# The low half of each weight gets a place of its own in the written order

## The reference, cut to what matters

```python
def reference(x, ...):
    x = first_block(x, ...)     # per layer: rms_norm, h @ w_in, two kinds of attention with
                                # relative bias, @ w_out, then conv_ffn (h @ w_up, causal
                                # conv of width 3, silu(g) * up, @ w_down)
    return second_block(x, ...) # per layer: adaptive rms_norm, h @ w_in of 15 sections (conv
                                # branch, attention with rope, gated linear attention with a
                                # chunked scan), three gated branches, @ w_out, rms_norm
```

## Time and profile before

| what | value |
|---|---|
| median of 3 executions | 2046.79 us (2045.48 to 2047.96) |
| the profiled execution | 2051.6 us |
| its span, first to last instruction | 2049.8 us |
| mean granted TensorE clock | 0.996 |
| TensorE busy | 2009.4 us (98%) |
| VectorE busy | 1330.0 us (65%) |
| ScalarE busy | 955.7 us (47%) |
| GpSimd busy | 159.3 us (8%) |

### The profile page before, as it was taken

One profiled execution on the slowest core, in us unless ns is written; L12 is line 12 of the kernel. 1 busy time (PEld: TensorE's weight loads), 2 busy tenths in 40 slices (PEclk: granted clock), 3 DMA queues, 4 the chain that ended last, 5 costly groups with the idle time before them and its releaser, 6 DMA issues.

```text
span 2049.8 us, 33452 instructions
## 1 busy us (share of the span) xinstructions
PE 2009.4 (98%) x13114; PEld 1738.3 (85%) x13114; DVE 1330.0 (65%) x2339; ACT 955.7 (47%) x1574; POOL 159.3 (8%) x169
## 2 busy tenths in 40 slices
PE   9999999999999999999999999999999999999998
PEld 7779998878999888888888788888878899888997
DVE  6767667767877337476445555868566686575665
ACT  4655555565555434353432453233246454445444
POOL 2001000000110100000200001111110000100100
PEclk9999999999999999999999999999999999999999
DMA  8446665535555322222222104534234244441554
GB/s 248 148 142 245 228 225 196 181 108 175 186 176 191 137 93 81 75 83 83 72 93 93 52 31 157 193 116 161 92 129 154 93 135 155 134 154 57 193 172 134
DMA packets 79706, 285.54 MB, mean 139 GB/s; under 512 B 8976, under 2 KB 9644, under 8 KB 79552
## 3 DMA queue, kind: packets, MB, share of 16 engines
q1 hardware_dynamic: 71136, 256.93, 37.7%
q10 hardware_dynamic: 6416, 19.51, 2.7%
q0 software_dynamic: 2000, 6.97, 1.3%
HBM read 277.55 MB, written 5.83 MB: 138 GB/s over the span
## 4 chain that ended last, share of the span: by engine, by line
PE 81%; DVE 10%; ACT 6%; issue 2%; DMA 1%; POOL 0%; ACTq 0%; DVEq 0%; SPq 0%
PE pb L1124 16%; PE pb L1126 15%; PE pb L1125 15%; PE pb L1137 6%; PE pb L1139 6%; PE pb L1138 6%; DVE SPL L2222 3%; ACT SPH L1637 3%; PE pb L1143 3%; PE pb L1302 2%; PE pb L1496 2%; PE pb L1303 2%; PE pb L1304 2%; PE pb L1477 2%; PE pb L1391 1%
## 5 line engine op out<-in xcount | busy, mean ns | idle before, releaser
L2222 DVE TENSOR_TENSOR SPL<-RAW,SPH 128x1024 fp32r<-128x1024 f32 x460 | 558.9, 1232 | 367.2 <-ACT SPH L1637 343.4
L1637 ACT ACTIVATE SPH<-RAW 128x1024 fp32r<-128x1024 f32 x462 | 477.4, 1052 | 208.4 <-PE pb L1126 111.3
L1124 PE MATMUL pb<-HTH,SPH 128*128 128x256 f32 (+1 forms) x1304 | 447.0, 343 | 8.4 <-POOL HTL L2881 3.1
L1126 PE MATMUL pb<-HTH,SPL 128*128 128x256 f32 (+1 forms) x1304 | 437.9, 336 | 0.0
L1125 PE MATMUL pb<-HTL,SPH 128*128 128x256 f32 (+1 forms) x1304 | 437.5, 335 | 0.0
L1124 PEld LDWEIGHTS pb<-HTH,SPH 128*128 128x128 f32 x1304 | 247.8, 190 | 36.8 <-ACT HTH L1686 3.2
L1126 PEld LDWEIGHTS pb<-HTH,SPL 128*128 128x128 f32 x1304 | 247.8, 190 | 26.1
L1125 PEld LDWEIGHTS pb<-HTL,SPH 128*128 128x128 f32 x1304 | 248.0, 190 | 24.8
L1137 PE MATMUL pb<-SPH,HTH 128*128 128x512 f32 x640 | 254.6, 398 | 2.1 <-DVE SPL L2222 1.4
L1139 PE MATMUL pb<-SPL,HTH 128*128 128x512 f32 x640 | 249.9, 390 | 0.0
L1138 PE MATMUL pb<-SPH,HTL 128*128 128x512 f32 x640 | 249.8, 390 | 0.0
(11 more groups left out here) (297 smaller groups left out, 2853.2 us busy)
## 6 DMA issues: line engine op xcount, KB each, us to landing
RAW<-in_w_up SPq DMA_DIRECT2D x88, 512.0 KB, 4.5
RAW<-in_wa SPq DMA_DIRECT2D x64, 512.0 KB, 3.5
RAW<-in_w_in SPq DMA_DIRECT2D x48, 512.0 KB, 4.7
RAW<-in_wmg SPq DMA_DIRECT2D x48, 512.0 KB, 3.5
RAW<-in_wbr SPq DMA_DIRECT2D x48, 512.0 KB, 3.5
RAW<-in_w_down SPq DMA_DIRECT2D x44, 512.0 KB, 4.9
RAW<-in_w_ada SPq DMA_DIRECT2D x24, 512.0 KB, 4.7
ARAW<-in_w_ada ACTq DMA_DIRECT2D x24, 512.0 KB, 4.2
```

The source lines that it names most:

```text
L1124: T.matmul(o, wh[:, kt, :], xh[:, kt, n0:n1], start=kt == 0, stop=False)
L1126: m = T.matmul(o, wl[:, kt, :], xh[:, kt, n0:n1], start=False, stop=kt == 7)
L1637: A.activation(hi, raw, ACT.Copy, scale=1.0).then_inc(*act.tick(s["hi"], ("u", u)))
L2222: W.tensor_tensor(lo, raw, hi.bitcast(F32), SUB).then_inc(*dve.tick(s["lo_dve"], ("u", u)))
```

## The change

The step `split` is now ScalarE's alone. VectorE (and POOL, where a fetch is its) has a step `split_low`. `split_upto` still adds `split` where it did, and notes the fetch as pending. `get_w(u)` first adds the low halves that are pending from the fetch before (`lows()`), then calls `split_upto` in its later form, which leaves the new ones pending; if u itself is among them, they are added at once. Every other call of `split_upto` adds its low halves at its end, as before.

So the low half of a fetch that `get_w(u)` starts is written one fetch later: behind the products of fetch u and behind all steps up to the next `get_w`. The high halves, the loads and TensorE's steps keep their order. No instruction is added or taken away.

```diff
+        self.later, self.pending = True, []
...
+    def lows(self):
+        for u in self.pending:
+            self.add("split_low", u)
+        self.pending = []
+
+    def split_upto(self, n, later=False):
         while self.order is not None and self.splits <= n and self.splits < len(self.order):
             u = self.splits
             self.load_upto(u + NR - 1)
             if u not in self.loaded:
-                return
+                break
             if self.order[u][3] == "split":
                 q = self.nsplit % NS
                 if q in self.held:
-                    return
+                    break
                 self.held.add(q)
...
                 self.add("split", u)
+                self.pending.append(u)
             self.splits += 1
+        if not later:
+            self.lows()
...
         if self.order is not None:
             assert self.order[u] == (name, idx, cols, kind)
-            self.split_upto(min(u + NS + 1, self.limit))
+            self.lows()
+            self.split_upto(min(u + NS + 1, self.limit), self.later)
+            if u in self.pending:
+                self.lows()
         return u
...
-    does = {"start": start, "cs": cs, "lam": lam, "split": split, "ada_turn": ada_turn, ...
+    does = {"start": start, "cs": cs, "lam": lam, "split_low": split, "ada_turn": ada_turn, ...
...
-    does = {"start": start, "qk_turn": qk_turn, "split": split, "bias_rows": bias_rows, ...
+    does = {"start": start, "qk_turn": qk_turn, "split_low": split, "bias_rows": bias_rows, ...
```

More of the change, by code:

```diff
@@ L183, in load_upto @@
             self.loads += 1
-    def split_upto(self, n):
+    def lows(self):
[3 more added lines that the diff above has]
+    def split_upto(self, n, later=False):
         while self.order is not None and self.splits <= n and self.splits < len(self.order):
@@ L2797, in x_out @@
             *dve.tick(o, ("x", l, t)))
-    does = {"start": start, "cs": cs, "lam": lam, "split": split, "ada_turn": ada_turn, "adv": adv, "adv_end": adv_end,
+    does = {"start": start, "cs": cs, "lam": lam, "split_low": split, "ada_turn": ada_turn, "adv": adv, "adv_end": adv_end,
             "adv_fin": adv_fin, "stats": stats, "scale": scale, "prod": prod, "bias_rows": bias_rows, "mask": mask, "picks": picks,
@@ L2944, in x_back @@
                     ).then_inc(*pool.tick(s["x_back"]))
-    does = {"start": start, "qk_turn": qk_turn, "split": split, "bias_rows": bias_rows, "consts": consts, "ctx_in": ctx_in,
+    does = {"start": start, "qk_turn": qk_turn, "split_low": split, "bias_rows": bias_rows, "consts": consts, "ctx_in": ctx_in,
             "bias_back": bias_back, "prod": prod, "up": up, "keep": keep, "gnorm": gnorm,
```

## The result

The change makes the kernel slower. Measured: 2059.15 us (median of 4 executions, 2058.14 to 2064.08) against 2046.13 (median of 4, 2044.27 to 2047.96); the ratio is 1.007, with an interval of 1.0058 to 1.0082. I had forecast slower, but 2052 with a range up to 2059: 5.2 us of +13.0. The profiled execution of after took 2058.1 us, 6.5 more than that of before (2051.6), and that distance is only half of what the medians give; the experiments come back to it.

A forecast was written before the change was run, and what follows sets the result against it. TensorE, busy 98% of the span, was taken as the bound almost everywhere. Gains of -14.5 and losses of +19.8 gave +5.3 us, 2056.9 against the profiled execution or 2052 against the median, range 2044 to 2059.

The forecast's parts named there:

- Item (6): First section of layer 0: fetch 4's low half, behind `qk_sums` and `qk_scale`, stalls TensorE from 25.73 to 31.75, +6.0 us.
- Item (7): Low granted clock after the stall at layer 0's first section: +2.4 us, with ends 0 and 3.4.
- The sum: Whole kernel: gains -14.5 plus losses +19.8 make +5.3 us, so 2052 against the median; chance 0.55.
- Item (10): Feed-forward of layer 1: late low halves of fetches 165 (+1.7) and 168 (+2.7), four fetches behind `prod c0` +1.6 us.
- Item (5): Small places of both signs, under 0.5 us each, estimated to sum to -1.2 us.
- Item (8): First section of layer 1, where only one low half is held: +0.4 us.
- (9): Residual and norm of block 1, both layers: low half between residual and statistics delays TensorE, 0.8 each, +1.6 us.
- Item (11): Heads of block 2, layer 1: three low halves behind norm and rope steps, 0.1, 1.4 and 1.9 late, +3.4 us.
- The loads: Rival: late low halves of fetches 4 to 6 delay loads of 9 to 11; +3, so 2055 us; chance 0.17.
- More is given back: Rival: heads and feed-forward have more slack, gated stages gain more; 2044.4 at best, around 2045.5 us; chance 0.19.
- the order is not what decides: Rival: signals, not written places, set VectorE's times, so nothing moves, 2046.8 us; chance 0.07.
- POOL's port: Rival: TensorE waits for each of POOL's 44 second halves blocked at the shared port, +20, 2072 us; chance 0.02.

The follow-up runs named there:

- the second trace: Profile of the change timed again without an edit: 2059.7 us against 2046.68 for before, ratio 1.0058.
- experiment 5: Kernel before, with only the low halves of fetches 165 and 168 (feed-forward of layer 1) one fetch later: ratio 1.0042, +8.6 us.
- experiment 2: Kernel before, with only the low halves of fetches 4, 5 and 6 one fetch later: ratio 1.0031, +6.3 us.
- experiment 7: Kernel before, with only uses 28 to 35 and 146 to 153 (residual and norm before the feed-forward) one fetch later: ratio 1.0010, +2.0 us.
- experiment 8: Kernel before, with only uses 413 to 426 (heads of layer 1, block 2) one fetch later: ratio 1.0007, +1.4 us.
- experiment 9: Kernel before, with only uses 12 to 27 and 133 to 145 (attention of block 1) one fetch later: ratio 0.9971, -5.9 us.
- experiment 3: The change, with the low halves of fetches 4, 5 and 6 alone where they were: 2054.16 us, ratio 1.0039 against before.
- experiment 6: Kernel before, with the other low halves of layer 1's feed-forward (not fetches 165 and 168) one fetch later: ratio 1.0026, +5.3 us.
- the picked versions: Before, low halves later only in block 1's attention and parts of block 2: 2036.5 us, 0.9944; wider pick adding uses 274-296, 423-426: 2033.53, 0.9949.
- experiment 4: The change, with fetch 4's low half alone where it was: 2055.71 us, ratio 1.0055 against before.
- experiment 1: Kernel before timed again without an edit, giving its second trace: median 2046.8 us, ratio 1.0005.

## Why the prediction was right and wrong

**The sign and the largest item were right.** Item (6) said a stall of 6.0 us from the low half of fetch 4; it was 6.03. Item (7) said 2.4 for the clock; stall and clock together were forecast at 8.4 and measured at 8.4 to 8.7. The stretch of 6.83 us at 0.50 began 1.75 before the stall ended.

**The step that failed is "The sum", on the side of the losses.** The sum of +5.3 is 7.9 below what the second trace shows. The terms that were mis-sized, by that trace:
- Item (10), the feed-forward: 6.0 forecast, 9.0 measured. I gave `up` the first of two inputs instead of the second (waits of 2.1 and 3.4 instead of 1.7 and 2.7 in experiment 5), left out a wait inside `prod` (four times 0.8 instead of 0.4), and had no term for the low clock there.
- Item (5), the small places: -1.2 forecast, some +1.6 measured. This was an estimate without rows. The largest of them are three waits on low halves at fetches 376, 384 and 390 (1.5 us in the change's waits there, in place of 0.6 on `GW`). Experiments 2, 7 and 8, which leave these uses alone, have 0.0 between fetches 370 and 402; experiments 5 and 9, which leave them alone too, have +2.1 and +1.5, with a low-clock stretch of 3.41 us there.
- Items (8) and (9), first sections of layer 1, norms and what follows them in layer 0: 2.0 forecast, 4.7 measured (3.6 in the first trace, which lacks the low clock at 148.7). The mechanism of (9) was wrong: the loss is a raw load held back by a low half, seen as waits on DMA (1.4 and 1.1 us in layer 0 and at its end, of the 3.7 in all). Item (8) is a wait of 0.6 at fetch 124. I had written that the loads hang on the low halves, and then looked for the effect only at fetches 9 to 11.
- Item (11), the heads' late halves: 3.4 forecast; the lag climbs by 4.1. The row's +0.3 against my +1.0 is luck, as 1.6 of what comes back is a low-clock stretch of the trace of before (experiment 8).
- The start differs by +0.4, which is within what two executions differ by.
- The gains were nearly right: attention -5.9 forecast, -5.5 by the trace and -5.9 by the timing; gated stages -5.0 forecast, -5.8 measured. One of three waits on `AE` was to go; all three stayed (1.6 became 1.3 us). A round of the gated stages takes 2.83 instead of 3.50:

```profile
1903.27 1.22 DVE L2234 TENSOR_TENSOR SPL<-RAW,SPH 128x1024 fp32r<-128x1024 f32 x1
...
1906.10 1.22 DVE L2234 TENSOR_TENSOR SPL<-RAW,SPH 128x1024 fp32r<-128x1024 f32 x1
```

One reading of the prediction is worded wrongly, without harm: a fetch of the earlier trace rows has 12 products in all, four groups of three, and 12 times 0.23 is the 2.7 that the sum uses.

**The clock had one term and needed more.** Every execution is listed with its mean granted clock. The change's four and five executions have 0.9945 and 0.9954, before's have 0.9973 to 0.9976 in the three sets. That is 0.0021 to 0.0030 of 2050 us, so by my estimate the clock takes 4 to 6 us at most (part of a low stretch can fall on idle time) of the 13, where item (7) had 2.4.

**The first pair of traces would have hidden this.** Against 2051.6, +5.3 comes to 2056.9, near the 2058.1 of the profiled execution. That nearness is an accident: the reference was 4.9 us long, the sum 7.9 short. I noted that the execution was 4.8 above the median and did not ask what in it was particular.

**The rivals.** *The loads* at fetches 9 to 11 did not decide: the loads from 20 to 55 us landed after a median of 8.3 us instead of 10.5, and no product waited for them; but the same mechanism did cost in the adaptive part. *More is given back* and *the order is not what decides* are refuted by the result itself and by experiments 2, 3 and 5. *POOL's port* cost TensorE 0.5 us in two waits on `AL` (the longest 0.2), against none in the earlier trace rows and 20 in the rival; the instruction grew in at least half of the places (ns min/median/max):

```profile
L2903 POOL TENSOR_TENSOR AL<-FT,AH x44: 735/1203/1656, 163.5 to 681.2; 128x256 fp32r<-128x256 f32 x44
```

The median went from 737 to 1203 ns, and POOL's busy time from 159.3 to 197.2 us, so 38 where I had 20. How much one grows depends on where it meets the low half. VectorE's and POOL's rows at one meeting:

```profile
603.50 1.21 DVE L2234 TENSOR_TENSOR SPL<-RAW,SPH 128x1024 fp32r<-128x1024 f32 x1
```

```profile
603.66 1.66 POOL L2903 TENSOR_TENSOR AL<-FT,AH 128x256 fp32r<-128x256 f32 x1 [8.86 <-DVE XN L2331]
```

The low half had 1.06 us to go when POOL's instruction began, and that one ended 0.60 after it. In the 28 places where about 0.61 us were left, it also ended 0.60 after VectorE's instruction, which makes the 1.20; in six places where nothing of VectorE's was under way as it began, it took 0.74. The rule of the Trainium skill ("SBUF — State Buffer", section "SBUF: two separate sides") said just that: the later of the two is blocked. The traces agree. It cost almost nothing because the hidden tiles are made well ahead.

**What stays open.** The medians of experiments 5 and 6 are 2.8 and 1.7 us above what their traces' steps show, at the edge of the interval (5) and inside it (6). For 5 the profiled execution was its shortest; for 6 it was its longest, and the cause isn't known. Nor is it known how much of the change's 13 us the clock takes in a given execution, beyond the estimate above. The places between 370 and 399 have no run of their own, nor have the gated stages; both are read from traces.

## What to carry to other kernels

Moving an instruction behind others on an in-order engine must be priced per place: by what the instructions passed wait for, not by their own length, and by the cover that the consumer's previous work gives (2.7 us per fetch here). Follow what the moved instruction frees as well, since a buffer that comes free later delays a load several fetches on. Where the profile names the last signal as what ended a wait, compare when both halves were ready before you believe the name. Before a sum is set against a median, take a second trace of the unchanged kernel: here two traces of one program differed by 4.9 us, as much as the effect that was forecast. And a mechanism that loses as a whole can win where it is applied by place: the picked versions are half a per cent faster than before.

## What the runs showed of the hardware

A wait of TensorE of 6.03 us came with 6.83 us at half the clock in all three traces that have such a wait (both of the change, experiment 2). In the change's first trace the stretch began 1.75 us before the wait ended. A wait of 3.3 us in experiment 4 was followed by none. After the wait of 3.4 us at 531 the change's first trace has a low stretch:

```profile
532.39:535.80 3.41, 3.41 (x18) 3.41 (x17) 0.95 (x1) 0.04 (x1) 0.00 (x0) 0.50 0.89 292
```

In its second trace the stretch stands at 520.8, behind the wait of 2.1 us there, and none follows the wait of 3.0 at 532.6:

```profile
520.79:524.20 3.41, 3.41 (x16) 3.31 (x16) 0.69 (x1) 0.50 (x2) 0.00 (x0) 0.50 0.79 281
```

So after waits of about 2 to 3.4 us it went either way here, and the same place in the same program fell in one execution and not in another (experiment 1). Where a stretch of 3.4 us can be read from the lag between two traces, it cost 1.3 to 1.6 us; a forecast for small stalls needs it as a range, not as a term.

In 37 of the 44 places of `AL` an instruction of VectorE, nearly always a low half, had 0.60 to 1.06 us left when POOL's began. Each of these POOL instructions ended 0.59 to 0.61 us after VectorE's, so their lengths run from 1.2 to 1.66.
